# Three small matmul groups of a compressed attention branch, issued by operand instead of alternating

## The reference

```python
nc = S // CMP_BLOCK                       # 1024 / 32 = 32 blocks
def compress(z, j):
    zb = z.reshape(B, nc, CMP_BLOCK, Dh) + pos_emb[j]
    return jax.nn.silu(zb.reshape(B, nc, CMP_BLOCK * Dh) @ w1[j]) @ w2[j]
kc = compress(k_cmp, 0)
vc = compress(v_cmp, 1)
s = jnp.einsum("bshd,bcd->bhsc", q, kc).astype(jnp.float32) * scale
s = s - slopes[:, None, None] * dist.astype(jnp.float32)
p_cmp = masked_softmax(s, dist >= 0)
o_cmp = jnp.einsum("bhsc,bcd->bshd", p_cmp.astype(vc.dtype), vc)
...
return g[..., 0:1] * o_cmp + g[..., 1:2] * o_sel + g[..., 2:3] * o_win
```

## Time and profile before

| | us |
|---|---|
| median of 3 executions | 2891.38 (2888.17 to 2892.67) |
| the profiled execution | 2888.17 |
| its span, first to last instruction | 2886.1 |
| TensorE busy | 2679.8 (93%) |
| VectorE, ScalarE, POOL busy | 923.9, 817.0, 873.4 |
| mean granted TensorE clock | 0.956 of full |

### The profile page before, as it was taken

The page is one execution under the profiler, slowest core; times in us unless marked ns, Lnnn a source line. Parts: engine busy times, 40 slices in busy tenths (PEclk is TensorE's granted clock), DMA queues, the critical chain, the costliest instruction groups (busy, mean ns, idle before and its releaser), DMA issues.

```text
span 2886.1 us, 30466 instructions
## 1 busy us (share of the span) xinstructions
PE 2679.8 (93%) x12660; PEld 2151.6 (75%) x12660; DVE 923.9 (32%) x1435; ACT 817.0 (28%) x1218; POOL 873.4 (30%) x492
## 2 busy tenths in 40 slices
PE   5899899999998999999999899798999999999896
PEld 5677677766677777778778677577888888888785
DVE  3312441133301444510227556413122222222423
ACT  2201442344322444431332333223211111111321
POOL 0211211344322211134542211235333323333633
PEclk9989999999999999999989899899999999999898
DMA  6101101100011000011203000120111111111111
GB/s 256 62 15 41 37 26 37 42 19 28 15 37 58 19 19 10 15 37 45 102 30 110 22 23 15 35 89 29 52 46 49 44 52 51 48 48 44 57 37 68
DMA packets 33432, 134.84 MB, mean 47 GB/s; under 512 B 3536, under 2 KB 3856, under 8 KB 32400
## 3 DMA queue, kind: packets, MB, share of 16 engines
q1 hardware_dynamic: 32976, 131.85, 13.2%
q10 hardware_dynamic: 320, 1.05, 0.1%
HBM read 123.45 MB, written 8.39 MB: 46 GB/s over the span
## 4 chain that ended last, share of the span: by engine, by line
PE 86%; DVE 6%; ACT 3%; POOL 2%; issue 2%; DMA 1%; SPq 0%; POOLq 0%; ACTq 0%; DVEq 0%
PE slot L654 54%; PE slot L700 12%; PE ps L865 4%; PE ps L836 3%; PE ps L732 3%; PE ps L814 2%; PE ps L898 1%; PE ps L889 1%; PE ps L902 1%; PE ps L915 1%; DVE cacc L2069 1%; DMA mm<-xT 1%; POOL wlo L1469 1%; DVE ada_sum L2007 1%; PE ps L758 1%
## 5 line engine op out<-in xcount | busy, mean ns | idle before, releaser
L654 PE MATMUL slot<-xhi,whi 128*128 128x512 f32 x2192 | 715.6, 408 | 58.8 <-ACT zs L1200 16.9
L654 PE MATMUL slot<-xlo,whi 128*128 128x512 f32 x2192 | 691.6, 397 | 0.0
L654 PE MATMUL slot<-xhi,wlo 128*128 128x512 f32 x2192 | 689.4, 396 | 0.0
L1469 POOL TENSOR_TENSOR wlo<-raw,whi 128x1024 fp32r<-128x1024 f32 (+1 forms) x169 | 428.7, 2536 | 860.0 <-ACT whi L1109 860.0
L654 PEld LDWEIGHTS slot<-xhi,whi 128*128 128x128 f32 x2192 | 405.9, 193 | 148.3 <-issue 65.8
L654 PEld LDWEIGHTS slot<-xlo,whi 128*128 128x128 f32 x2192 | 421.3, 192 | 92.1
L654 PEld LDWEIGHTS slot<-xhi,wlo 128*128 128x128 f32 x2192 | 420.6, 192 | 91.8
L1109 ACT ACTIVATE whi<-raw 128x1024 fp32r<-128x1024 f32 (+1 forms) x169 | 186.1, 1101 | 322.9 <-PE slot L700 174.5
L700 PE MATMUL slot<-uhi,whi 128*128 128x512 f32 x512 | 158.3, 390 | 0.0
L700 PE MATMUL slot<-ulo,whi 128*128 128x512 f32 x512 | 157.8, 389 | 0.0
L700 PE MATMUL slot<-uhi,wlo 128*128 128x512 f32 x512 | 157.6, 389 | 0.0
(11 more groups left out here) (308 smaller groups left out, 3103.7 us busy)
## 6 DMA issues: line engine op xcount, KB each, us to landing
raw<-wstream SPq DMA_DIRECT2D x129, 512.0 KB, 3.2
raw<-wstream SPq DMA_DIRECT2D x40, 640.0 KB, 3.9
ada<-wada SPq DMA_DIRECT2D x6, 2048.0 KB, 15.7
mm<-xT SPq DMA_DIRECT2D x1, 4096.0 KB, 23.7
mm<-xT SPq DMA_DIRECT2D x8, 512.0 KB, 4.4
res_dram<-mm SPq DMA_DIRECT2D x8, 512.0 KB, 4.1
res<-res_dram SPq DMA_DIRECT2D x8, 512.0 KB, 6.5
outT<-res SPq DMA_DIRECT2D x8, 512.0 KB, 2.6
```

The lines of the kernel that those rows point to most:

```text
L654: o = mm_(outs[:, half * HALF:(half + 1) * HALF], w[b % 2][:, k_w, :], x[:, k_x, half * HALF:(half + 1) * HALF], start=first and j == 0, s ...
L1469: tt(flat(wlo[b % 2])[:, 0:n], raw[:, 0:n], flat(whi[b % 2])[:, 0:n].bitcast(F32), ALU.subtract).then_inc(w_lo, 1)
```

## The change

In step 0 all 32 matmuls of the keys now come before the 32 of the values. In step 2 the heads come one after the other, 0 and 2, then 1 and 3, with the ordered wait between the pairs. In step 4 the four banks are given up for one, `ps7`: the heads are computed one after the other, each head in four pairs of matmuls, one pair for each quarter of the partitions, with an ordered wait between the pairs. After each head VectorE writes it to `ytok` in one product of 512 columns and raises `c_y`, for which TensorE's next head waits. The numbers of matmuls stay the same in all three steps; VectorE has four products of 512 columns in place of eight of 256.

```diff
--- before.py
+++ after.py
@@ -466,7 +466,6 @@
         ps7 = psum("ps7", [P, HALF])
         psb = [ps4[:, 0:HALF], ps4[:, HALF:S]]
         skz = [psb[0], psb[1], ps6]
-        cmp_banks = [psb[0], psb[1], ps6[:], ps7[:]]
 
         res_dram = nc.dram_tensor("res_dram", [P, NC, S], F32, kind="Internal").ap()
 
@@ -922,9 +921,9 @@
                 if s == 0:
                     pe.wait_ge(cmp_in, 32)
                     pe.wait_ge(c_pos, 1)
-                    zts = [acmp[j * DH:(j + 1) * DH, :].rearrange("d (c l) -> d l c", l=32) for j in range(2)]
-                    for l in range(32):
-                        for j, zt in enumerate(zts):
+                    for j in range(2):
+                        zt = acmp[j * DH:(j + 1) * DH, :].rearrange("d (c l) -> d l c", l=32)
+                        for l in range(32):
                             o = mm_(psb[j][0:DH, 0:NCMP], cw1s[j * DH:(j + 1) * DH, l, :], zt[:, l, :],
                                     start=l == 0, stop=l == 31)
                     o.then_inc(c_h, 1)
@@ -937,15 +936,14 @@
                     pe.wait_ge(c_kvs, 2)
                     wait_evacuated(pe, "Aq0")
                     wait_evacuated(pe, "Aq1")
-                    for first in (0, 2):
-                        if first:
+                    for h in (0, 2, 1, 3):
+                        if h == 1:
                             ordered(o)
+                        r0 = DH * (h % 2)
                         for i in range(NB):
-                            for h in (first, 3 - first):
-                                r0 = DH * (h % 2)
-                                c = h * NB * NCMP + i * NCMP
-                                o = mm_(ps4[:, c:c + NCMP], brq[r0:r0 + DH, h // 2, i * P:(i + 1) * P],
-                                        kct[r0:r0 + DH, :], start=True, stop=True)
+                            c = h * NB * NCMP + i * NCMP
+                            o = mm_(ps4[:, c:c + NCMP], brq[r0:r0 + DH, h // 2, i * P:(i + 1) * P],
+                                    kct[r0:r0 + DH, :], start=True, stop=True)
                     o.then_inc(c_s, 1)
                 elif s == 3:
                     pe.wait_ge(c_p, 1)
@@ -959,12 +957,17 @@
                         o.then_inc(c_t, 1)
                 elif s == 4:
                     pe.wait_ge(c_tb, 2)
-                    for c in range(2 * H):
-                        for g in range(4):
-                            o = mm_(cmp_banks[g][:, c * DH:(c + 1) * DH], pbuf[1][32 * g:32 * g + 32, c * P:(c + 1) * P],
-                                    vc4[32 * g:32 * g + 32, :], start=True, stop=True, tile_position=(32 * g, 0))
-                            if c == 2 * H - 1:
-                                o.then_inc(c_o, 1)
+                    for h in range(H):
+                        if h:
+                            pe.wait_ge(c_y, h)
+                        for i in (0, 4, 1, 5, 2, 6, 3, 7):
+                            if 0 < i < 4:
+                                ordered(o)
+                            r0 = 32 * (i % 4)
+                            c = (h * 2 + i // 4) * P
+                            o = mm_(ps7[:, i * DH:(i + 1) * DH], pbuf[1][r0:r0 + 32, c:c + P],
+                                    vc4[r0:r0 + 32, :], start=True, stop=True, tile_position=(r0, 0))
+                        o.then_inc(c_o, 1)
 
             def forget_prep(s):
                 if s == 0:
@@ -1975,15 +1978,11 @@
                 elif s == 4:
                     wait_evacuated(dve, "turned Ag1")
                     wait_tile(dve, TILE["yC1"])
-                    dve.wait_ge(c_o, 4)
-                    for g in range(4):
-                        for a in range(2):
-                            i = 4 * a + g
-                            part = cmp_banks[g].rearrange("p (h a d) -> p h a d", h=H, a=2)[:, :, a, :]
-                            gate = gates[:, i, :].rearrange("p (h k) -> p h k", k=3)[:, :, 0:1]
-                            ins = v.tensor_tensor(ytok[:, i, :].rearrange("p (h d) -> p h d", h=H), part,
-                                                  gate.to_broadcast([P, H, DH]), ALU.mult)
-                        ins.then_inc(c_y, 1)
+                    for h in range(H):
+                        dve.wait_ge(c_o, h + 1)
+                        v.tensor_tensor(ytok[:, :, h * DH:(h + 1) * DH], ps7[:].rearrange("p (b d) -> p b d", b=NB),
+                                        gates[:, :, 3 * h:3 * h + 1].to_broadcast([P, NB, DH]), ALU.mult
+                                        ).then_inc(c_y, 1)
 
             dve.wait_ge(small_in, 32)
             link(v.tensor_copy(identb[:], t_("ident")))
```

## The result

| | before | after |
|---|---|---|
| median, first series | 2889.78 us (4 runs) | 2918.87 us (4 runs, 2916.25 to 2926.74) |
| ratio, first series | | 1.0104 [1.0083, 1.0126] |
| median, second series | 2889.61 us (11 runs) | 2915.50 us (6 runs, 2911.68 to 2922.27) |
| ratio, second series | | 1.0090 [1.0076, 1.0105] |
| the profiled execution, its span | 2888.17, 2886.1 us | 2915.78, 2913.8 us |

The account below looks back on a forecast made before the run. TensorE, in order and busy 93% of the span, was taken as the bound. 6.7 + 5.5 + 14.4 - 3.4 = +23.2 us gave 2911.4 from the profiled 2888.17, or 2914.6 against the median; range 2906 to 2922.

Parts of the forecast that it names:

- The price of a row group: Steps 0, 2, 4: groups run side by side, each with a 0.11 us period at full clock for 128-column loads.
- Rival C: All three steps: loads in one row group run ahead into a spare weight buffer; +2.0 us, 2893.4; chance 0.05.
- Step 0: Compression step 0: one group at a time at half clock, 13.75 us against 7.04, +6.7; bounds 0 and +8.0.
- Step 2: Compression step 2: 7.5 us plus 2.0 for a clock fall some 5 us in, +5.5; bounds +3.5 and +10.
- Step 4 to the unit: Step 4's start to the first selection unit: 22.6 us against 8.20, +14.4; bounds +9.0 and +17.
- the step that named the releaser: Behind step 4: VectorE's last product, then its 2.83 us key split, releases the first selection unit.
- The start of the selection: First selection units: full clock instead of half, 9.3 us shrink to 5.9, -3.4; bounds 0 and -3.4.
- Behind the region: After the selection's start: the sum had no further term, so 0 us.
- The clock: Half through step 0, falling some 5 us into step 2 and in step 4's second head; full in the selection.
- Rival A: Steps 2 and 4: the clock holds through both; +15.8 us, 2907.2; chance 0.20.
- Rival B: Steps 0, 2 and 4: the clock is lost for longer, no return; +35 us, 2926.4; chance 0.12.

Follow-up runs that it names:

- sixth kernel: Kernel before with only step 2 changed: heads 0 and 2 together, then 1 and 3, banks still alternating between matmuls; 2900.26 us, ratio 1.0032.
- fifth: Kernel before with step 4's 16 records of one row group issued before the next group's, four banks, no ordered waits; 2891.0 us, one run.
- tenth kernel: Kernel after with the dense parts moved as in the eighth kernel; 2905.91 us, ratio 1.0049 against the kernel before.
- step 2 alone: Kernel before with only the change's order of step 2 (heads 0, 2, then 1, 3); 2903.32 us, ratio 1.0041.
- step 2 twice: Kernel before with step 2's matmuls issued two times in the old order; 2896.86 us, ratio 1.0029.
- eighth kernel: Kernel before with dense parts moved: two ahead of step 0, five instead of two between steps 2 and 3, fewer elsewhere; 2873.21 us, ratio 0.9933.
- fourth kernel: Kernel before with step 4 head by head and ordered waits, but each head in its own bank, no waits for VectorE between heads; 2897.21 us, ratio 1.0021.

## Why the prediction was right

**The price of a row group: right.** The prediction's period came from four loads in retention, 0.11 us each. Step 2's first half took 3.70 us where 3.7 was worked out. The sixth kernel shows that the partitions make it, not the bank, and the fifth shows a period of 0.11 for quarters too. Rival C, the background buffer, needed a period under 0.06 and is ruled out for these operands. What the 0.116 us consist of (load, passage, hand-over) no run here separates.

**Step 0: +6.4 us, forecast +6.7.** 13.43 us, twice measured in the kernel after and once alone. The clock did stay at half through the step, as forecast, and rose as long after its end as before, so that neither bound was needed.

**Step 2: +5.45 us, forecast +5.5.** 9.47 us against 4.02. The fall of the clock, put some 5 us into the step, came after 5.4. The upper bound was met in the tenth kernel: all at half is 14.12 us (bound: 14). No kernel kept the clock through the step in its new order, so the lower bound was not seen.

**Step 4 to the unit: +14.6 us, forecast +14.4; right sum, one term wrong, and some luck.** The heads follow each other after 3.67, 4.75 and 5.39 us (forecast 3.6, 5.0, 5.6), and the last takes 4.61 (4.8): 18.4 us against 19.0. Behind them the prediction put VectorE on the path, with 2.83 us for the key split. It took 1.22. The 2.83 of the earlier trace rows was measured while POOL had three operations beside it, from 945.22 to 951.87 in the profile before; in the changed kernel POOL was idle for 17.8 us at this point. All traces agree: the split takes 2.82 to 2.84 us in the six where POOL works beside it, and 1.21 or 1.22 in the eight where POOL is idle. POOL's own last subtraction, which released the unit before, took 1.44 us beside the split and 0.45 without it. The release then came from TensorE's own queue, twelve dense matmuls in 4.49 us, of which the prediction had said only that this path is about as long. By VectorE's path the unit could have started near 977.2. So the step that named the releaser failed. By the prediction's own rows TensorE's path came to 18.7 + 2 x 2.86 = 24.4 us at half clock, more than the 22.6 that it went by. The time held by luck: the heads were 0.6 us shorter than forecast, and what followed them 0.8 longer (4.42 against 3.63).

**The start of the selection: -3.9 us, forecast -3.4.** At the unit the kernel after was 27.7 us late (979.69 against 952.01), at the dense matmuls of the fourth full-clock unit 23.8 (993.14 against 969.35). The region began 0.5 us later in it. 6.4 + 5.45 + 14.6 - 3.9 = 22.6, and 0.7 lies between the transposes (step 3) and step 4, where the half clock behind the idle lasted longer: 23.3 us against the 23.2 of the sum.

**Behind the region: 0 forecast.** In the first execution 4 us more came, in the second next to none (23.7 us at the end). They come from falls of the clock in the window attention that differ between executions of the same kernel, as those of the kernel before do by 2 us. Whether the change has any share in them on average stays open: the medians differ by 25.9 and 29.1 us in the two series, above the region's 23.3 in both. Other kernels leave the same question: step 2 alone is 10.7 us slower by medians and 5.9 longer in the region, its twin with alternating banks 7.6 and 5.8, and step 2 twice 6.5 and 6.5.

**The clock: right for its result.** Rival A held the clock through steps 2 and 4, for step 2 has dense work on both sides. The tenth kernel put more of it ahead of step 0 and behind step 2, and the clock fell 2.5 us into step 0. Rival B had the clock gone with no return; it returned 2.9 us behind the end of step 0 (921.0 to 923.9) and some 3.3 us behind that of step 4. In the tenth kernel something like it happened: no return for 34 us, from 911.2 to 945.3. That dense work brings the clock back within some 3 us is therefore what this stretch showed, not a rule. The eighth kernel shows the counterpart: the old order at full clock keeps it through steps 0 and 2, which last 3.93 and 4.02 us. Step 2 twice shows the limit of that: at 10.4 us the old order loses it too.

The Trainium skill ("TensorE: Matmul & The Clock Gate", Part 3), in the sentence that a weight load overlaps with running matmuls only if its row group differs, agrees with what these kernels show: side by side across row groups, one after the other within one.

## What to carry to other kernels

Matmuls that fill a half or a quarter of the rows should alternate their row groups. Without that each record costs its group's whole period (0.116 us here at full clock) instead of about a half or a quarter of it, and the longer stream that results can lose the clock although TensorE shows as busy. A bank shared by successive groups costs more than the wait for the engine that empties it, since it also ends the overlap between neighbours. A duration read beside a busy POOL isn't that of the same instruction alone, so before an engine is put on the path, ask what its neighbour will be doing in the changed order. And where two paths come out within 2 us of each other, work out both.

## What the runs showed of the hardware

- The period of one record with 128 weight columns in one row group is 0.116 us at full clock over 32 records of step 2 (3.70 / 32), and 0.220 at half (7.04 / 32 in the tenth kernel); two groups side by side give about half of that (2.00 us for 32 records), four about a quarter (2.01 us for 64).
- With 64 weight columns and two groups side by side, 128 records take 3.93 us at full clock and 7.04 at half, a ratio of 1.79.
- With 64 weight columns in one group, the period is 0.058 us at full clock (41 records in the first 2.4 us of step 0 in the tenth kernel) and 0.106 at half (13.43 us for 128).
- A VectorE subtraction of 128x1024 from SBUF took 2.83 us with POOL busy and 1.22 with POOL idle.
- The second group of four in another partition quarter and another bank came nearly free in the fourth kernel: eight records in 1.18 us, four in 1.12, at half clock.
- An ordered wait and four records make 0.71 us at full clock and 1.17 at half (957.56 to 958.27, and 963.38 behind 962.21, in the chain of the kernel after).
- The granted clock fell under streams of small records with TensorE busy: after 5.4 us in step 2 of the kernel after, 2.5 in step 0 of the tenth kernel, 5.2 in step 2 twice. It stayed full through 3.93 and 4.02 us of them in the eighth.
- In two executions of the kernel after, the clock falls alike up to 1101 us (but for one fall in an idle time) and then differs (10.1 us at half from 1125.4 in the first only); their spans are 4 us apart.
